# Norms of a two-block transformer kernel: turning scaled rows in place of a matmul with a diagonal

## The reference

```python
def rms_norm(x, g):
    xf = x.astype(jnp.float32)
    y = xf * lax.rsqrt(jnp.mean(xf * xf, axis=-1, keepdims=True) + EPS)
    return (y * g.astype(jnp.float32)).astype(x.dtype)

def swiglu(h, w_in, w_out):
    gate, up = jnp.split(h @ w_in, 2, axis=-1)
    return (jax.nn.silu(gate) * up) @ w_out
```

## Time and profile before

| | |
|---|---|
| median of 3 runs | 3321.71 us (3320.27 to 3321.99) |
| profiled execution, its own time | 3322.24 us |
| its span in the trace | 3320.5 us |
| PE busy | 3163.5 us, 95% |
| DVE busy | 1877.7 us, 57% |
| ACT busy | 1471.5 us, 44% |
| chain that ended last | PE 90%, DVE 6%, ACT 2%, issue 1%, DMA 1% |

### The profile page before, as it was taken

One profiled execution on the slowest core, in us unless ns is written; L12 is line 12 of the kernel. 1 busy time (PEld: TensorE's weight loads), 2 busy tenths in 40 slices (PEclk: granted clock), 3 DMA queues, 4 the chain that ended last, 5 costly groups with the idle time before them and its releaser, 6 DMA issues.

```text
span 3320.5 us, 52983 instructions
## 1 busy us (share of the span) xinstructions
PE 3163.5 (95%) x22719; PEld 2991.1 (90%) x22719; DVE 1877.7 (57%) x2529; ACT 1471.5 (44%) x2265; POOL 78.9 (2%) x153
## 2 busy tenths in 40 slices
PE   8999999999999997999999999988889999888999
PEld 8989999989989997998989998987779999777897
DVE  5555555556545557555556655585655456664554
ACT  4455444444434443444445544434344443443443
POOL 0000000000000000000000000000000000000000
PEclk9999999999999998999999999988899998888999
DMA  6563555554555552555555355741235565313354
GB/s 211 190 206 106 183 180 183 186 193 159 187 186 183 185 183 71 163 187 184 179 187 187 130 182 187 201 147 35 100 115 178 187 190 176 104 64 114 127 179 139
DMA packets 434398, 533.92 MB, mean 161 GB/s; under 512 B 27330, under 2 KB 398452, under 8 KB 434164
## 3 DMA queue, kind: packets, MB, share of 16 engines
q1 hardware_dynamic: 421220, 512.22, 47.7%
q10 hardware_dynamic: 12944, 18.31, 1.6%
HBM read 528.33 MB, written 1.11 MB: 159 GB/s over the span
## 4 chain that ended last, share of the span: by engine, by line
PE 90%; DVE 6%; ACT 2%; issue 1%; DMA 1%; POOL 0%; SPq 0%; DVEq 0%; POOLq 0%; ACTq 0%
PE bank L670 88%; PE bank L870 1%; DVE sb_parts L1521 1%; DMA sb_o_rows<-in_mem_dram 0%; DVE sb_sc L1669 0%; ACT sb_prT L1109 0%; PE bank L708 0%; DVE sb_oT_low L1609 0%; ACT sb_oT_high L1072 0%; ACT sb_sc L1193 0%; DVE sb_tmp L1853 0%; DVE sb_nmax L1671 0%; DVE sb_arena L1856 0%; DMA sb_ring<-in_ff_w_in_dram 0%; ACT sb_parts L1098 0%
## 5 line engine op out<-in xcount | busy, mean ns | idle before, releaser
L1521 DVE TENSOR_TENSOR sb_parts<-sb_ring,sb_parts 128x2048 fp32r<-128x2048 f32 (+1 forms) x480 | 1098.4, 2292 | 653.5 <-ACT sb_parts L1098 652.6
L670 PE MATMUL bank<-sb_hT_high,sb_parts 128*128 128x256 f32 x7888 | 1431.4, 284 | 6.7 <-DVE sb_hT_low L1607 5.4
L670 PEld LDWEIGHTS bank<-sb_hT_high,sb_parts 128*128 128x128 f32 x7888 | 1237.2, 193 | 8.3 <-DVE sb_hT_low L1607 6.2
L1098 ACT ACTIVATE sb_parts<-sb_ring 128x2048 fp32r<-128x2048 f32 (+1 forms) x480 | 912.5, 1908 | 583.7 <-PE bank L670 496.0
L670 PE MATMUL bank<-sb_hT_low,sb_parts 128*128 128x256 f32 x3944 | 1119.7, 284 | 0.0
L670 PEld LDWEIGHTS bank<-sb_hT_low,sb_parts 128*128 128x128 f32 x3944 | 760.1, 193 | 0.0
L670 PE MATMUL bank<-sb_parts,sb_hidden_high 128*128 128x512 f32 x1760 | 544.0, 390 | 0.0
L670 PE MATMUL bank<-sb_parts,sb_hT_high 128*128 128x256 f32 (+2 forms) x2432 | 458.2, 291 | 21.8 <-DVE sb_hT_low L1619 10.0
L670 PEld LDWEIGHTS bank<-sb_parts,sb_hT_high 128*128 128x128 f32 x2432 | 392.5, 199 | 28.1 <-DVE sb_hT_low L1619 17.5
L670 PEld LDWEIGHTS bank<-sb_parts,sb_hidden_high 128*128 128x128 f32 x1760 | 329.8, 188 | 74.5 <-issue 0.6
L1158 ACT ACTIVATE sb_prT<-bank 128x256 f32<-128x256 f32 x220 | 84.6, 385 | 636.3 <-PE bank L670 636.3
(11 more groups left out here) (203 smaller groups left out, 2137.9 us busy)
## 6 DMA issues: line engine op xcount, KB each, us to landing
sb_ring<-in_ff_w_in_dram SPq DMA_DIRECT2D x176, 1024.0 KB, 5.1
sb_ring<-in_ff_w_out_dram SPq DMA_DIRECT2D x88, 1024.0 KB, 5.0
sb_ring<-in_w_gate_up_dram SPq DMA_DIRECT2D x44, 1024.0 KB, 5.1
sb_ring<-in_w_in_dram SPq DMA_DIRECT2D x42, 1024.0 KB, 5.3
sb_ring<-in_a_w_qkv_dram SPq DMA_DIRECT2D x24, 1024.0 KB, 5.2
sb_ring<-in_w_down_dram SPq DMA_DIRECT2D x22, 1024.0 KB, 4.9
sb_ring<-in_c_w_qkv_dram SPq DMA_DIRECT2D x12, 1024.0 KB, 5.2
sb_ring<-in_a_w_o_dram SPq DMA_DIRECT2D x8, 1024.0 KB, 5.2
```

What stands on the lines that cost most here:

```text
L670: return nc.tensor.matmul(o, lhsT, rhs, start=start, stop=stop)
L1098: nc.scalar.activation(halves(n, slice(0, filled(n))).high, ring[:, raw_in[n], 0:filled(n)], ACT.Copy) \
L1521: V.tensor_tensor(both.low, ring[:, raw_in[n], 0:filled(n)], both.high.bitcast(F32), ALU.subtract) \
```

## The change

Step 3 and 4 are replaced. When the factor is ready, DVE scales columns 512 to 1023 of the tile and ACT scales columns 0 to 511, both from x into `xn`. PE waits for both and turns `xn` with the transposing form against the identity. ACT's half stands in its list behind the squares of x of the same tile. The memory's own norm keeps its diagonal. The small tables at the start move from `xn` to a part of `o_rows`, since `xn` is now written at the start.

```diff
@@ names
         tmp2 = xn[:, 1, 512:1024]
+        steps = o_rows[:, 1, 0:512]
@@ TensorE, norm_tile
                 pe.wait_ge(rows_ready.sem, rows_ready.at((n, t)))
+                pe.wait_ge(act_step.sem, act_step.at((n, t, "rows")))
                 for b in range(KD // 2):
                     bank = (G, YB)[t].take(pe, (n, t, b))
                     for kt in (2 * b, 2 * b + 1):
-                        ins = mm(bank[:, (kt % 2) * P:(kt % 2 + 1) * P], x[:, t, kt * P:(kt + 1) * P], diag[:, t, :], True, True)
+                        ins = nc.tensor.transpose(bank[:, (kt % 2) * P:(kt % 2 + 1) * P], xn[:, t, kt * P:(kt + 1) * P], ident[:, :])
@@ ScalarE
+            def scaled_rows(n, t):
+
+                act.wait_ge(rstd_ready.sem, rstd_ready.at((n, t)))
+                copy(xn[:, t, 0:512], x[:, t, 0:512], rstd[:, 2 + t:3 + t]).then_inc(act_step.sem, act_step.next((n, t, "rows")))
+
@@ ScalarE, turn: behind the squares of x of tile t
                             squares(x[:, t, h * 512:(h + 1) * 512], 4 + 2 * t + h, (norm_after(st), t, h))
+                    if follows and follows != "final":
+                        scaled_rows(follows, t)
@@ ScalarE, start of the program: behind the squares of tile t
                     squares(x[:, t, h * 512:(h + 1) * 512], 4 + 2 * t + h, ((stages[0], "norm"), t, h))
+                scaled_rows((stages[0], "norm"), t)
@@ VectorE
-            def row_factor(n, t, d0=0):
+            def row_factor(n, t, d0=None):
 
                 mean_of_halves(n, t, 2 + t, 4 + 2 * t, (n, t))
                 dve.wait_ge(rstd_ready.sem, rstd_ready.at((n, t)))
-                V.tensor_scalar(diag[:, d0 + t, :], ident[:, :], rstd[:, 2 + t:3 + t], None, ALU.mult) \
-                    .then_inc(rows_ready.sem, rows_ready.next((n, t)))
+                if d0 is None:
+                    ins = V.tensor_scalar(xn[:, t, 512:D], x[:, t, 512:D], rstd[:, 2 + t:3 + t], None, ALU.mult)
+                else:
+                    ins = V.tensor_scalar(diag[:, d0 + t, :], ident[:, :], rstd[:, 2 + t:3 + t], None, ALU.mult)
+                ins.then_inc(rows_ready.sem, rows_ready.next((n, t)))
```

More of the change, by code:

```diff
@@ L1441, in _ @@
             step(pool.memset(minus_half[:, :], -0.5))
-            step(pool.iota(tmp2[0:BUCKETS, 0:16], pattern=[[1, 16]], base=0, channel_multiplier=0,
+            step(pool.iota(steps[0:BUCKETS, 0:16], pattern=[[1, 16]], base=0, channel_multiplier=0,
                            allow_small_or_imprecise_dtypes=True), "exact")
-            step(pool.iota(tmp2[0:BUCKETS, 16:17], pattern=[[0, 1]], base=0, channel_multiplier=1,
+            step(pool.iota(steps[0:BUCKETS, 16:17], pattern=[[0, 1]], base=0, channel_multiplier=1,
                            allow_small_or_imprecise_dtypes=True), "bucket")
@@ L2063, in set_up_lines @@
                 step(V.memset(buckets, -1.0))
-                step(V.tensor_copy(buckets[:, P:P + 16], tmp2[0:BUCKETS, 0:16]))
+                step(V.tensor_copy(buckets[:, P:P + 16], steps[0:BUCKETS, 0:16]))
                 for b in range(16, BUCKETS):
@@ L2067, in set_up_lines @@
                     step(V.memset(buckets[:, P + ds[0]:P + ds[-1] + 1], float(b)))
-                step(V.tensor_scalar(onehot[:, :], buckets, tmp2[0:BUCKETS, 16:17], None, ALU.is_equal), "onehot")
+                step(V.tensor_scalar(onehot[:, :], buckets, steps[0:BUCKETS, 16:17], None, ALU.is_equal), "onehot")
             def set_up_angles():
```

## The result

The changed kernel takes 3329.14 us (median of 12 runs, 3323.93 to 3334.66); the kernel before, run beside it, takes 3321.32 us (12 runs, 3318.90 to 3322.42). The ratio is 1.0025, with a 95% interval of 1.0016 to 1.0034: slower by 7.8 us. The profiled execution took 3328.8 us and its span is 3327.1, 6.6 more than before.

What follows compares the result with a forecast made beforehand. TensorE, busy 95% of the span, was taken to bound the kernel, time counting where it stands. Terms -4.4 + 5.5 + 2.0 + 2.9 + 1.0 + 4.5 = +11.5 gave 3333.2 us, range 3324 to 3343.

Steps and rivals of the forecast that it cites:

- rival (c): TensorE's work counts everywhere: 288 records fewer save 32 us, giving 3289.7 us, faster; chance 0.04.
- TensorE's part: Turning takes one record instead of two; only the first bank counts, 0.23 us at 19 tiles, -4.4 us.
- Rival (e): The transposing form takes two records for this data after all, so 4.4 us is not won: 3337 us; chance 0.03.
- ACT's half row: Tile 0's half row delays tile 1's squares: +0.69 us behind eight feed-forwards (+5.5), +0.50 behind four mixers (+2.0).
- Its next work, a gain product, waits for ACT's square anyway: DVE's scaling grows from 0.29 to about 0.49 us, but lies beside ACT's longer half everywhere: costs nothing.
- The nineteenth tile: Tile 1 ahead of the first branch stage, counted among 19 tiles gaining 0.23 us; later gain-row loads cost nothing.
- The memory load: At two memory blocks, ACT issues the load 1.44 us later, behind tile 1's scaled row: +2.9 us, bounds 0 to 3.5.
- rival (b): Memory load's delay is taken up, its landing set by traffic, and no clock fall: +4.1, 3325.8 us; chance 0.15.
- The start: ACT scales both tiles before its first weight split, 12.6 instead of 10.75; partly repaid: +1.0 us (0.6 to 1.5).
- The clock: Longer TensorE idling at twelve places halves the clock at three, 1.5 us each: +4.5 us, between 0 and 18.
- (a): No clock fall behind the twelve gain stages: +7.0 us, 3328.7 us; chance 0.20.
- (d): The clock falls in all twelve places: +7.0 + 18, 3346.7 us; chance 0.08.

Runs made afterwards that it cites:

- filled gap: Changed kernel, with TensorE turning tile 0's last two blocks five times instead of once behind the twelve gain stages; 3324.52 us, ratio 1.0014.
- half row alone: Kernel before plus ACT's scaled half row, which nobody reads, and TensorE's wait for it; 3327.91 us, ratio 1.0028.
- all on DVE: Changed kernel, but DVE scales all 1024 columns, ACT makes no half row and TensorE waits for DVE alone; 3315.48 us, ratio 0.9992.
- second profile of the changed kernel: Changed kernel run again unaltered, on another comparison's chip; 3329.36 us, ratio 1.0033 to the kernel before.
- the load first: Changed kernel, with ACT issuing the memory-row load ahead of tile 1's half row; 3328.52 us, ratio 1.0029 to the kernel before.
- two steps on DVE: Whole rows scaled on DVE in two instructions, TensorE starting on the first 256 columns; 3315.87 us, ratio 0.9991 to the kernel before.

## Why the prediction came out as it did

**What bounds the kernel: right.** TensorE gave up 29 us of work and the kernel became slower. In the filled gap 96 passes more cost nothing, which says the same from the other side. That disposes of rival (c).

**TensorE's part: right.** One record per turning, 0.23 us for the first bank in 18 of 19 tiles. Rival (e) falls with the 288 records.

**ACT's half row: the mechanism right, each place a little undersized.** The square starts 0.63 behind the factor and the last one 0.76 behind it (forecast 0.62 and 0.77). The sum was +7.5 and is +8.65, for two reasons. The step "Its next work, a gain product, waits for ACT's square anyway" failed: with the squares close together DVE's two products become the last link, 0.07 a place. And at one feed-forward (1201 us) the factor comes 0.35 us later than elsewhere, so that even TensorE's turning waits 0.51 us: +1.10. The kernel before shows the same lateness. It arises on DVE: at 1196.24 its second step of the mean starts 0.46 after the end of ACT's sum (1195.59 + 0.19), elsewhere 0.11 after it (210.71 behind 210.42 + 0.19). What holds it is not shown.

**The nineteenth tile: a cost at "nothing" that was not.** "The loads of gain rows, issued behind the last squares, go later by about 1.4 us and are needed a stage later: nothing" forgot the other DMAs in that place. Ahead of the first branch stage ACT issues four, and in its queue they now stand between the half row and hT_high:

```profile
2076.02 0.72 ACT L1074 ACTIVATE sb_xn<-sb_x,sb_rstd 128x512 f32<-128x512 f32 x1 [0.93 <-POOL sb_rstd L1445]
2076.08 0.38 ACTq L1267 DMA_DIRECT2D sb_arena<-line_dram  x1
2076.49 1.13 ACTq L1272 DMA_DIRECT2D sb_arena<-in_cmp_w_k_dram  x2
2077.65 0.56 ACTq L1272 DMA_DIRECT2D sb_arena<-in_cmp_w_v_dram  x1
2078.25 2.17 ACT L1074 ACTIVATE sb_hT_high<-bank,sb_gT 128x128 fp32r<-128x128 f32 x8 [1.51 <-PE bank L719]
```

The row names TensorE as what ended the wait, but TensorE had been turning since 2077.28; hT_high starts when the last issue is over (2077.65 + 0.56 = 2078.21). TensorE restarts 0.33 us later than before instead of 0.23 earlier. In the kernel with the half row alone it is +0.67, and with all on DVE -0.23.

**The memory load: wrong, the step that failed.** The step is "so the issue moves from 2414.36 to 2415.80, +1.44" and, from it, "Two such blocks: +2.9". The issue did move, by 1.39 against tile 0's turning. The landing did not: 11.20 for 11.53. The forecast carried the delay of the issue through to the landing as if the transfer took a fixed time. The runs show that the load's packets begin when those of the weight chunks ahead of them run out, 7.2 to 7.5 us behind the start of the turning for every issue between 3.34 and 5.20. The lower bound, 0, was the nearer end; measured are -0.39 for both blocks, and the 0.33 by which two profiles of the changed kernel differ in this landing shows that a minus of this size can be chance. That part of rival (b) is what happened. The prediction had also named a memory turning that is not later as a sign of being wrong, and this sign came: 24.71 for 25.04, with 4.49 us of idleness ahead of it for 4.30, not about 2 us more.

**The start: right.** ACT's first weight split moved from 10.75 to 12.80 (forecast 12.6) and hT_low from 17.84 to 19.15, 1.31 for 1.15. It leaves +0.87 after the half clock has paid some back. That figure is of one execution: TensorE restarts 1.29 later in the second profile of the changed kernel, and +0.29 are left of it there, +1.30 with the load first. The forecast of +1.0 lies between them. ACT's rows at the start:

```profile
8.87 0.72 ACT L1074 ACTIVATE sb_xn<-sb_x,sb_rstd 128x512 f32<-128x512 f32 x1 [1.01 <-POOL sb_rstd L1445]
...
11.88 0.72 ACT L1074 ACTIVATE sb_xn<-sb_x,sb_rstd 128x512 f32<-128x512 f32 x1 [0.93 <-POOL sb_rstd L1445]
...
12.80 1.91 ACT L1100 ACTIVATE sb_parts<-sb_ring 128x2048 fp32r<-128x2048 f32 x1
```

**The clock: right in kind, the count a lucky choice.** Forecast were three falls of 1.5 us. The traces have two, three and three, each of 1.48 to 1.51 us. The 1.5 was worked out; the three was picked between 0 and 12 with no row that gave it. Rivals (a), none, and (d), twelve, are both out by the traces. By the time alone (a) would have won: its 3328.7 lies nearer to the measured 3329.14 than the forecast does, because it left out 3.0 us of falls and charged 2.9 us for a memory load that cost nothing. In the filled kernel the granted clock stays at 1.00 in all twelve places, and what fills the gap there is turning by the identity alone. The rule weighed ahead of the result, that a transposing pass does not count as activity (the Trainium skill, TensorE: Matmul & The Clock Gate, Part 4), would have the filled kernel fall as often as the changed one; this case's traces speak against it, with 0 of 12 to 8 of 36. The evidence is thin, though: if eight falls lay by chance in these 48 places, the twelve of the filled kernel would be spared about one time in twelve.

**The sum.** Taken from the terms, forecast +11.5, the differences are -3.3 for the memory load, -1.5 for the clock, +1.15 for the gain places, +0.56 for the branch stage's tile, -0.13 for the start, +0.1 for the first bank's rounding, and -1.84 from half clock elsewhere: +6.6, the difference of the spans. If the last part averages out over many runs, the terms are +8.4; the medians say +7.8 in the main comparison and +10.2 in the repetition. So the hit is in part luck: a term of +2.9 that does not exist and a third fall stood against places and a tile that cost 1.7 more than forecast.

## What to carry to other kernels

Before work is moved to an engine that looks idle, read what stands behind it in that engine's queue: 0.72 us on ACT cost 8.7 us over twelve places, not for its length, but because its wait for the factor went ahead of squares that used to run while TensorE was finishing. The same instruction one place later in the queue cost nothing. A shorter piece of TensorE's work gives only what its first bank gives to the chain behind it; the rest becomes idle time, and idle time beside a light load can cost clock. And a load's issue time says little about its landing while other loads are under way: look at when its packets begin before a delay is charged.

## What the runs showed of the hardware

- A load of 1 MB issued 1.4 us later took 6.2 us to land instead of 8.0, with the DMA engines busy at 0.90 in both. Its packets began 7.29 and 7.30 us behind the start of the turning, when those of the weight loads on another queue ran out; in 18 blocks of nine profiles, with issues from 3.34 to 5.20, they began between 7.17 and 7.45.
- The twelve places are alike to 0.03 us in two profiles of one kernel, yet only one of them fell to half clock in both (1205.1 and 1203.8); the others differ (1362.1; 1552.0 and 1876.2). Each stretch lasted 3.4 us.
- 96 extra passes of TensorE into idle gaps cost nothing, and the clock stayed at 1.00 in all twelve places.
- DVE scales 512 columns of f32 in 0.49 us, 1024 in 0.75, and 256 in 0.35: one instruction over twice the columns is far below two.
- Four DMA issues on ACT's queue, 2.1 us in all (2076.08 to 2078.21), hold up its next computation although none of them computes.

Open: why the factor is 0.35 us late at one feed-forward's end in eight of the nine profiles and not with two steps on DVE; why the clock fell there in all three profiles with the longer gap; and whether any part of "elsewhere" belongs to the change. By their medians the two forms on DVE alone are the best of all, 3 to 4 us below the kernel before, but their intervals reach 1.0: no version here is clearly faster than the kernel before.
